# A fused two-block transformer kernel on Trainium2: the second convolution's products joined, high and low halves of the activations through one stationary block

## The chip, the cores and the metric

The kernel runs on one core of one Trainium2 chip. The metric is the device time of one execution in microseconds (us). Engines are named TensorE (PE, its weight loads PEld), VectorE (DVE), ScalarE (ACT), GpSimd (POOL) and SyncE (SP, which issues the weight DMAs).

## What is computed

The reference runs two transformer blocks over 256 tokens of width 1024, all in float32. The change lies in the second block, which is (cut):

```python
u = rms_norm(x, norm1_g[l])
proj = u @ w_in[l]
q, k, v, cb, cc, ch, ga, gb = jnp.split(proj, split_pts, axis=-1)   # cb, cc, ch: 512 columns each
...
y_a = neighbourhood_attention(q, k, v, rpb[l]) @ w_attn_branch[l]
y_b = short_gated_conv(cb, cc, ch, conv_w[l]) @ w_conv_branch[l]
merged = jax.nn.sigmoid(ga) * y_a + jax.nn.sigmoid(gb) * y_b
...
def short_gated_conv(cb, cc, ch, w):
    z = cc * ch
    zp = jnp.pad(z, ((0, 0), (1, 1), (0, 0)))
    conv = zp[:, :-2] * w[0] + zp[:, 1:-1] * w[1] + zp[:, 2:] * w[2]
    return cb * conv
```

## The kernel before, in words

Every float32 product is made of three products of a faster 32-bit type: both operands are split into a high part (rounded) and a low part (the rest), and high x high, high x low and low x high are summed in PSUM. ScalarE makes the high part of each weight piece (`split_hi`, L1105) and VectorE the low part (`split_lo`, L1524).

The weights stream through in 147 pieces of 128x2048 (1 MB), numbered by slot `s`. Each slot is one step of a loop that every engine runs over all slots, in program order; what an engine does in a slot stands in its block of code, and semaphores tie the engines. A piece is split two slots ahead (`AHEAD`), in rings of three buffers. The order around the change, in slots: q2 87 and 88, k2 89 and 90, v2 91 and 92, **cb2 93 and 94, cc2 95 and 96, ch2 97 and 98**, then four chunks of gates g2 (99 to 106), then the branch products ab2, cv2. A chunk of 512 columns takes two pieces, each over half of the 1024 input features; the first *opens* the PSUM banks and the second *closes* them.

PSUM has eight banks of 512 float32 words in each partition. `claim(key, b)` makes TensorE wait until bank `b` was drained by its last reader (semaphore `bank_drained<b>`); `ready` makes a reader wait until a bank was filled; `drain_of` counts it as drained. cb2, cc2 and ch2 have the form "feat" (features on the partitions): four tiles of 128 features x 256 tokens, two tiles in a bank. `stream` runs a piece in two halves, one bank each, with 24 matmuls of 256 columns per half (`three`, L402: weight high x activation high, weight high x activation low, weight low x activation high). Bank pairs (0, 1) and (2, 3) alternate by chunk: `b = 2 * pair[0] + half`, and `pair[0] ^= 1` when a chunk closes. cb2 so lies in banks 2 and 3, cc2 in 0 and 1, ch2 in 2 and 3, the first gates chunk in 0 and 1.

Between the two halves of a piece, `slot_middle` puts in the attention of the second block: a score block (`scores`, L801, banks 4 and 5) in slots 94 to 97 and a value block (`values2`, L838, bank 7) in slots 97 to 100, and after the pieces 96 to 99 a turn block (`prob_turn`, L816, banks 6 and 7). On VectorE the attention is `softmax_max` (L1696 reads banks 4 and 5 and adds the bias, L1701 takes the maximum), `softmax_divide` (L1717, L1719) and the low part `o_lo` of the values (L2109, which drains bank 7); on ScalarE it is `exps` (L1184), `prob_out` (L1216) and `o_hi` (L1474).

VectorE evacuates cb2 and cc2 (L2080: a bank half times the row scale) after `split_lo` of its slot and before the slot's `softmax_max`, and ch2 (L2130: z2 = ch2 x cc2) as the last of slot 98, after that slot's `softmax_divide`.

The MLP pieces have the form "wide" (`stream_wide`, L586 and L591): one stationary block of weights meets the high and low halves of the activations side by side, 512 columns, in one bank; then the low part of the weights meets the high activations, 256 columns, into the bank's first half. The two halves of a bank are added afterwards: ScalarE copies the second halves of two banks (L1227), VectorE adds the first halves (L1901).

Of the kernel before, what the change touches and what calls it, by code (L numbers as in the profile page):

```python
# [29 lines left out]
ALU = mybir.AluOpType  # L30
# [3 lines left out]
P = 128  # L34
# [78 lines left out]


TURN_AT = {18: 0, 19: 1, 20: 2, 21: 3, 22: 4, 24: 5}
SILU_AT = {19: (2, 3), 21: (4,), 23: (5,), 25: (6,)}
TAPS_AT = {9: 0, 13: 1, 15: 2, 17: 3, 19: 4, 21: 5, 23: 6, 25: 7}
LAST_TAPS = 26
# [37 lines left out]
def build(nc, w_stream, w_kv, x_in, params_in, table_in, onehot_in, gate_bias_in, post_in, rpb_in,  # L156
# [3 lines left out]
    with ctx:  # L160
# [154 lines left out]
        def sem(name):  # L315
            return ctx.enter_context(nc.semaphore(name))
# [19 lines left out]
        conv_tap0, conv_tapped, conv_silu, z_first_silu = (  # L336
            sem("conv_tap0"), sem("conv_tapped"), sem("conv_silu"), sem("z_first_silu"))
        z_last_silu, skip_ready = sem("z_last_silu"), sem("skip_ready")
        cum_ready = sem("cum_ready")
        ndt_ready = sem("ndt_ready")  # L340
        decay_scaled, own_ready, x_state_ready = sem("decay_scaled"), sem("own_ready"), sem("x_state_ready")
# [25 lines left out]
        def emptied(eng, key):  # L367

            eng.wait_ge(drained[where[key][0]], where[key][1] + 1)
# [12 lines left out]
        def _(pe):  # L382
            def claim(key, b):

                if uses[b]:
                    pe.wait_ge(drained[b], uses[b])
                where[key] = [b, uses[b], None]
                uses[b] += 1

            def fill_of(key):  # L390

                b = where[key][0]
                fills[b] += 1
                where[key][2] = (filled[b], fills[b])
                return filled[b], 1

            def three(o, act_hi, act_lo, hi, lo, weights_still, first, last):
# [3 lines left out]
                for n, (still, moving) in enumerate(pairs):  # L401
# [7 lines left out]
            hi_first = {"wo": (12, "mix0"),  # L409
                        "wo2": (24, "mix1"), "mi2": (28, "norm3")}  # L410
            crossed = ("wo", "mo", "wo2", "mo2")
            pair = [0]

            def stream_hi_first(s):
# [156 lines left out]
                    where[("q", 0, 1)][2] = (piece_done, 2)  # L571
                    pair[0] ^= 1

            def stream_wide(s):

                name, form, chunk, part, opens, closes = slots[s]
                hi, lo = w_hi[s % SPLIT_RING], w_lo[s % SPLIT_RING]

                def cols(kt, i):
                    return slice(kt * 512 + i * P, kt * 512 + i * P + P)  # L580

                def highs(i):
                    if opens:
                        claim((name, chunk, i), 4 * (chunk % 2) + i)
                    for kt in range(4):
                        pe.matmul(ps[:, 4 * (chunk % 2) + i, :], hi[:, cols(kt, i)], ht[:, :, 4 * part + kt, :],  # L586
                                  start=opens and kt == 0, stop=False, skip_group_check=True)

                def lows(i):
                    for kt in range(4):  # L590
                        ins = pe.matmul(ps[:, 4 * (chunk % 2) + i, 0:TOK], lo[:, cols(kt, i)],  # L591
                                        ht_hi[:, 4 * part + kt, :], start=False, stop=closes and kt == 3,
                                        skip_group_check=True)
                    return ins

                together = 2 if closes else 4
                for first in range(0, 4, together):
                    for i in range(first, first + together):
                        highs(i)
                    if first == 0:  # L600
                        pe.wait_ge(lo_ready, s + 1)
                    for i in range(first, first + together):
                        ins = lows(i)
                        if closes and i < 3:
                            ins.then_inc(*fill_of((name, chunk, i)))
                ins.then_inc(piece_done, 1)
                if closes:
                    where[(name, chunk, 3)][2] = (piece_done, s + 1)
# [32 lines left out]
            def stream(s, between=None):  # L641
# [1 line left out]
                hi, lo = w_hi[s % SPLIT_RING], w_lo[s % SPLIT_RING]  # L643
                pe.wait_ge(hi_ready, s + 1)
                if form == "wide" and chunk:
                    stream_wide(s)
                    return
                pe.wait_ge(lo_ready, s + 1)
                if name in hi_first and chunk == 0 and form != "acc":
# [437 lines left out]
        def _(act):  # L1087
# [168 lines left out]
            for s in range(SLOTS):  # L1256
# [213 lines left out]
                if 0 <= s - 97 < 4:  # L1470
                    a = s - 97
                    r, g = a // 2, a % 2
                    ready(act, ("a2o", a))
                    act.activation(o2_hi[:, 2 * g:2 * g + 2, r * P:r * P + P],  # L1474
                                   ps[:, 7, 0:2 * P].rearrange("p (h i) -> p h i", h=2),
                                   ACT.Copy).then_inc(ot_hi_ready, 1)
                if 0 <= s - 96 < 4:
                    prob_out("a2", s - 96, 0, prob_t2)
                    prob_out("a2", s - 96, 1, prob_t2)
                if s == S_CH2 + 2:  # L1480

                    emptied(act, ("ch2", 0, 0)), emptied(act, ("ch2", 0, 1))
                    for i in range(4):
                        act.activation(acc2[:, i, :], z2[:, i, 1:1 + TOK], ACT.Copy,
                                       scale=conv_w2[:, 1, i:i + 1]).then_inc(tap2_ready, 1)
# [3 lines left out]
                if name == "g2" and closes:  # L1489
                    for r in range(RT):  # L1490
                        key = ("g2", chunk, r)
                        ready(act, key)
                        if chunk == 0 and r == 0:

                            act.wait_ge(prob_ready, 12)
                            emptied(act, ("cb2", 0, 1)), emptied(act, ("cc2", 0, 1))
                        act.activation(gates2[:, r, chunk * 512:chunk * 512 + 512], ps[:, bank(key), :],
                                       ACT.Sigmoid, scale=row_scale[:, 0, r:r + 1]).then_inc(*drain_of(key))
                if s == S_WO2 - 1:
# [12 lines left out]
        def _(dve):  # L1512
# [381 lines left out]
            def feed_forward(name, c):  # L1894
# [11 lines left out]
                for half in range(2):  # L1906
# [2 lines left out]
                    dve.tensor_tensor(ff_lo[:, f:f + 2, :], ff_sum[half][:, :, :],  # L1909
                                      ff_hi[:, f:f + 2, :].bitcast(F32), ALU.subtract).then_inc(ff_ready, 1)  # L1910

            def mix(j, dest, first, second):

                for r in range(RT):
                    for n in range(2):
                        a = dest[:, r, n * 512:n * 512 + 512]
                        b = dest[:, r, D + n * 512:D + n * 512 + 512]
                        key = (second, n, r)
                        ready(dve, key)
                        own, other = (a, b) if j == 0 else (b, a)  # L1920
                        dve.tensor_tensor(own, ps[:, 2 * n + r, :], own, ALU.mult).then_inc(*drain_of(key))
                        emptied(dve, key)
                        emptied(dve, (first, n, r))
                        dve.tensor_tensor(a, a, b, ALU.add).then_inc(mixed_ready, 1)  # L1924
# [26 lines left out]
            for s in range(SLOTS):  # L1951
# [123 lines left out]
                if name in ("cb2", "cc2") and closes:  # L2075
                    dest, power = (cb2, 0) if name == "cb2" else (cc2, 1)
                    for half in range(2):
                        key = (name, 0, half)
                        ready(dve, key)
                        dve.tensor_tensor(dest[:, 2 * half:2 * half + 2, :],  # L2080
                                          ps[:, bank(key), :].rearrange("p (a b) -> p a b", a=2),
                                          scale_row[:, power, :].unsqueeze(1).to_broadcast([P, 2, TOK]),
                                          ALU.mult).then_inc(*drain_of(key))

                if name in ("q2", "k2") and closes:
                    part_of = 0 if name == "q2" else 1
# [34 lines left out]
                    softmax_divide(s - 95, logit2, 8, False)  # L2121

                if name == "ch2" and closes:
                    emptied(dve, ("cc2", 0, 0)), emptied(dve, ("cc2", 0, 1))
                    dve.wait_ge(pads_zero, 2)
                    for half in range(2):
                        key = ("ch2", 0, half)
                        ready(dve, key)
                        f = slice(2 * half, 2 * half + 2)
                        dve.tensor_tensor(z2[:, f, 1:1 + TOK],  # L2130
                                          ps[:, bank(key), :].rearrange("p (a b) -> p a b", a=2),
                                          cc2[:, f, :], ALU.mult).then_inc(*drain_of(key))
                if s == S_CH2 + 3:
                    for i in range(4):
                        dve.wait_ge(tap2_ready, i + 1)
                        for tap in (0, 2):
                            link(dve.scalar_tensor_tensor(acc2[:, i, :], z2[:, i, tap:tap + TOK],
                                                          conv_w2[:, tap, i:i + 1], acc2[:, i, :],
                                                          ALU.mult, ALU.add))
                    emptied(dve, ("cb2", 0, 0)), emptied(dve, ("cb2", 0, 1))  # L2140
                    dve.tensor_tensor(acc2[:, :, :], acc2[:, :, :], cb2[:, :, :], ALU.mult).then_inc(conv2_ready, 1)
                if s == S_CH2 + 4:
                    dve.wait_ge(co_hi_ready, 1)
# [209 lines left out]
```

## Time and profile before

| | us |
|---|---|
| median of 3 runs (lowest to highest) | 931.22 (930.92 to 931.59) |
| the profiled execution's own time | 930.91 |
| its span in the trace | 929.1 |
| TensorE busy | 922.3 (99%) |
| weight loads busy | 798.5 (86%) |
| VectorE busy | 656.6 (71%) |
| ScalarE busy | 522.7 (56%) |
| GpSimd busy | 59.1 (6%) |
| DMA share of 16 engines, hardware queue | 47.2% |

The span is the traced part of the profiled execution; the sum of the prediction is made against that execution. Matmuls are pipelined: a matmul's own duration is longer than the distance to the start of the next, so their pace is read from starts, and from counts over a stretch.

### The profile page before, as it was taken

The numbers are of one execution on the slowest core, as the hardware profiler recorded it, in microseconds if no ns is written. First come the engines' busy times: TensorE is split into PE (matmuls) and PEld (weight loads), VectorE is DVE, ScalarE is ACT, GpSimd is POOL, SyncE is SP. The second block draws the span as 40 slices with busy tenths as digits, with TensorE's granted clock in tenths as the row PEclk, the third lists the DMA queues.
The fourth block names the chain that finished last, engine by engine and source line by source line (L and its number), as shares of the span: only waits on it lengthen the run. The fifth ranks groups of instructions, "written<-read, shape, count | busy, mean of one in ns | idle before, by whom it ended". The sixth has DMA issues, their size and how long they took to land.

```text
span 929.1 us, 13131 instructions
## 1 busy us (share of the span) xinstructions
PE 922.3 (99%) x5264; PEld 798.5 (86%) x5264; DVE 656.6 (71%) x972; ACT 522.7 (56%) x735; POOL 59.1 (6%) x59
## 2 busy tenths in 40 slices
PE   9999999999999999999999999999999999999998
PEld 7988999988888888888888888899888898888886
DVE  6669989988889655788775446768655768876333
ACT  7457787767874733665554335756644356554330
POOL 1000000112231000000004400000000000000000
PEclk9999999999999999999999999999999999999999
DMA  8943334453227575445557854553355445455541
GB/s 308 369 147 127 101 127 142 177 166 128 91 91 249 171 281 181 181 171 184 196 194 224 255 186 177 181 181 137 136 184 206 168 139 210 182 186 222 187 176 46
DMA packets 25277, 166.51 MB, mean 179 GB/s; under 512 B 2986, under 2 KB 3114, under 8 KB 6912
## 3 DMA queue, kind: packets, MB, share of 16 engines
q1 hardware_dynamic: 22464, 156.12, 47.2%
q0 software_dynamic: 2752, 9.54, 3.4%
q8 instruction: 42, 0.69, 0.3%
q14 instruction: 19, 0.16, 0.0%
HBM read 164.57 MB, written 1.08 MB: 178 GB/s over the span
## 4 chain that ended last, share of the span: by engine, by line
PE 93%; DVE 4%; ACT 2%; issue 1%; DMA 0%; SPq 0%; DVEq 0%; ACTq 0%
PE ps L402 60%; PE ps L586 11%; PE ps L591 6%; PE ps L517 2%; PE ps L872 1%; PE ps L801 1%; PE ps L816 1%; PE ps L918 1%; PE ps L665 1%; PE ps L524 1%; PE ps L892 1%; PE ps L881 1%; PE ps L826 1%; DVE conv_acc L1783 1%; DVE gates L1924 1%
## 5 line engine op out<-in xcount | busy, mean ns | idle before, releaser
L1524 DVE TENSOR_TENSOR w_lo<-raw,w_hi 128x2048 fp32r<-128x2048 f32 (+1 forms) x144 | 330.1, 2297 | 183.6 <-ACT w_hi L1105 183.6
L1105 ACT ACTIVATE w_hi<-raw 128x2048 fp32r<-128x2048 f32 (+1 forms) x144 | 274.0, 1906 | 186.7 <-PE ps L402 160.2
L402 PE MATMUL ps<-w_hi,ht 128*128 128x512 f32 (+1 forms) x576 | 183.3, 390 | 0.0
L402 PE MATMUL ps<-ht,w_hi 128*128 128x256 f32 x800 | 148.1, 286 | 0.0
L402 PEld LDWEIGHTS ps<-ht,w_hi 128*128 128x128 f32 x800 | 124.3, 191 | 4.6 <-issue 4.6
L402 PEld LDWEIGHTS ps<-w_hi,ht 128*128 128x128 f32 x576 | 107.6, 188 | 22.3 <-issue 1.0
L402 PE MATMUL ps<-ht,w_lo 128*128 128x256 f32 x400 | 113.1, 283 | 0.0
L402 PE MATMUL ps<-w_lo,ht 128*128 128x512 f32 (+1 forms) x288 | 111.0, 385 | 0.0
L586 PE MATMUL ps<-ht,w_hi 128*128 128x512 f32 x448 | 109.6, 391 | 0.0
L402 PE MATMUL ps<-w_hi,ff_hi 128*128 128x512 f32 x256 | 99.7, 389 | 0.0
L402 PE MATMUL ps<-w_lo,ff_hi 128*128 128x512 f32 x256 | 99.6, 389 | 0.0
L402 PE MATMUL ps<-w_hi,ff_lo 128*128 128x512 f32 x256 | 99.6, 389 | 0.0
L586 PEld LDWEIGHTS ps<-ht,w_hi 128*128 128x128 f32 x448 | 81.5, 189 | 15.2
L402 PEld LDWEIGHTS ps<-ht,w_lo 128*128 128x128 f32 x400 | 76.6, 191 | 0.0
L402 PEld LDWEIGHTS ps<-w_lo,ht 128*128 128x128 f32 x288 | 54.1, 188 | 10.4
L591 PEld LDWEIGHTS ps<-ht,w_lo 128*128 128x128 f32 x448 | 59.3, 191 | 3.3
L591 PE MATMUL ps<-ht,w_lo 128*128 128x256 f32 x448 | 60.3, 282 | 0.0
L402 PEld LDWEIGHTS ps<-w_hi,ff_lo 128*128 128x128 f32 x256 | 48.1, 188 | 10.1
L402 PEld LDWEIGHTS ps<-w_lo,ff_hi 128*128 128x128 f32 x256 | 48.1, 188 | 9.9
L402 PEld LDWEIGHTS ps<-w_hi,ff_hi 128*128 128x128 f32 x256 | 48.1, 188 | 9.8
L1783 DVE SCALAR_TENSOR_TENSOR conv_acc<-conv_in,params,conv_acc 128x256 f32<-128x256 f32 x128 | 52.0, 481 | 0.0
L1227 ACT ACTIVATE ff_sum<-ps 128x512 f32<-128x512 f32 x30 | 17.8, 596 | 37.7 <-PE ps L591 36.9
(305 smaller groups left out, 1200.7 us busy)
## 6 DMA issues: line engine op xcount, KB each, us to landing
raw<-in_w_stream SPq DMA_DIRECT2D x143, 1024.0 KB, 4.8
bias<-rel_scratch POOLq DMA_DIRECT2D x1, 3072.0 KB, 22.6
bias<-in_rpb POOLq DMA_DIRECT2D x16, 128.0 KB, 8.3
raw<-in_w_kv SPq DMA_DIRECT2D x2, 864.0 KB, 8.4
x_first<-in_x_in SPq DMA_DIRECT2D x2, 512.0 KB, 4.0
raw<-in_w_stream SPq DMA_DIRECT2D x2, 512.0 KB, 6.2
gates<-in_gate_bias POOLq DMA_DIRECT2D x4, 256.0 KB, 5.6
gates<-in_gate_bias POOLq DMA_DIRECT2D x2, 512.0 KB, 7.7
```

What stands on the lines that cost most here:

```text
L402: ins = pe.matmul(o, still, moving, start=first and n == 0, stop=last and n == 2, skip_group_check=True)
L517: pe.matmul(ps[:, bank0 + r, :], ht_hi[:, 4 * part + kt, tokens], w[:, kt * 512:kt * 512 + 512], start=part == 0 and kt == 0 and m == 0, s ...
L524: ins = pe.matmul(ps[:, bank0 + r, :], ht_lo[:, 4 * part + kt, tokens], hi[:, kt * 512:kt * 512 + 512], start=False, stop=part == 1 and kt ...
L586: pe.matmul(ps[:, 4 * (chunk % 2) + i, :], hi[:, cols(kt, i)], ht[:, :, 4 * part + kt, :], start=opens and kt == 0, stop=False, skip_group ...
L591: ins = pe.matmul(ps[:, 4 * (chunk % 2) + i, 0:TOK], lo[:, cols(kt, i)], ht_hi[:, 4 * part + kt, :], start=False, stop=closes and kt == 3, ...
L665: pe.matmul(ps[:, 2 * n + r, :], a_hi[:, kt, r * P:r * P + P], w[:, cols], start=kt == 0 and m == 0, stop=False, skip_group_check=True)
L801: ins = pe.matmul(ps[:, 4 + e, h * TOK:h * TOK + TOK], q_tile(h)[rows, (1 - r) * P:(1 - r) * P + P], k_tile(h)[rows, :], start=True, stop= ...
L816: ins = pe.transpose(ps[:, 6 + half, o:o + P], logit[a % 2][:, 2 * half + h, jt * P:jt * P + P], flip)
L1105: act.activation(split_home(s)[0][:, 0:width(s)], raw[s % RAW_RING][:, 0:width(s)], ACT.Copy).then_inc(hi_ready, 1)
L1227: act.activation(ff_sum[half][:, :, :], ps[:, b:b + 2, TOK:2 * TOK], ACT.Copy).then_inc(lows_out, 1)
L1524: dve.tensor_tensor(lo[:, 0:width(s)], raw[s % RAW_RING][:, 0:width(s)], hi[:, 0:width(s)].bitcast(F32), ALU.subtract).then_inc(lo_ready, 1)
L1783: ins = dve.scalar_tensor_tensor(acc_of(c)[:, i, :], conv_in[k][:, i, tap:tap + TOK], conv_w[:, tap, f:f + 1], acc_of(c)[:, i, :], ALU.mul ...
```

## The change

The three chunks cb2, cc2 and ch2 take the wide form: each chunk uses four banks (0 to 3), one for each tile of 128 features, 16 matmuls of 512 columns and 16 of 256 in a piece, in two halves of two banks with the attention block still between them. ScalarE copies the low halves of two banks into the chunk's own SBUF tile (cb2, cc2, or acc2 for ch2) and counts `later_lows`. VectorE's new `add_lows` adds the banks' first halves onto it, one instruction a bank, waits for their end, and then multiplies as before, now from SBUF. `conv_scaled` and `gated2` take the place of the bank counts that later readers waited for. The bank pair is no longer turned over by these three chunks. (`name == "q"` and `WIDE_Q` have no effect: q is not in `joined_later`.)

```diff
@@ tensor @@
+            joined_later = ("cb2", "cc2", "ch2",)
...
-            def stream_wide(s):
+            def stream_wide(s, bank_of, together, between=None):
...
                 def highs(i):
                     if opens:
-                        claim((name, chunk, i), 4 * (chunk % 2) + i)
+                        claim((name, chunk, i), bank_of(i))
                     for kt in range(4):
-                        pe.matmul(ps[:, 4 * (chunk % 2) + i, :], hi[:, cols(kt, i)], ht[:, :, 4 * part + kt, :],
+                        pe.matmul(ps[:, bank_of(i), :], hi[:, cols(kt, i)], ht[:, :, 4 * part + kt, :],
...
+                    if first == 0 and together == 2 and between:
+                        between(s)
...
                 if form == "wide" and chunk:
-                    stream_wide(s)
+                    stream_wide(s, lambda i: 4 * (chunk % 2) + i, 2 if closes else 4)
+                    return
+                if name in joined_later:
+                    stream_wide(s, lambda i: (WIDE_Q if name == "q" else range(4))[i], 2, between)
+                    if name == "q" and closes:
+                        pair[0] ^= 1
                     return
@@ scalar @@
+                if name in ("cb2", "cc2", "ch2") and closes:
+                    dest = {"cb2": cb2, "cc2": cc2, "ch2": acc2}[name]
+                    for half in range(2):
+                        ready(act, (name, 0, 2 * half)), ready(act, (name, 0, 2 * half + 1))
+                        act.activation(dest[:, 2 * half:2 * half + 2, :], ps[:, 2 * half:2 * half + 2, TOK:2 * TOK],
+                                       ACT.Copy).then_inc(later_lows, 1)
                 if 0 <= s - 96 < 4:
                     prob_out("a2", s - 96, 0, prob_t2)
...
                 if s == S_CH2 + 2:
-                    emptied(act, ("ch2", 0, 0)), emptied(act, ("ch2", 0, 1))
+                    act.wait_ge(gated2, 2)
...
-                            emptied(act, ("cb2", 0, 1)), emptied(act, ("cc2", 0, 1))
+                            act.wait_ge(conv_scaled, 4)
@@ vector @@
+            def add_lows(name, dest, half, first):
+                dve.wait_ge(later_lows, first + half + 1)
+                for i in range(2 * half, 2 * half + 2):
+                    key = (name, 0, i)
+                    dve.tensor_tensor(dest[:, i, :], ps[:, bank(key), 0:TOK], dest[:, i, :],
+                                      ALU.add).then_inc(*drain_of(key))
+                emptied(dve, (name, 0, 2 * half)), emptied(dve, (name, 0, 2 * half + 1))
...
                     for half in range(2):
-                        key = (name, 0, half)
-                        ready(dve, key)
-                        dve.tensor_tensor(dest[:, 2 * half:2 * half + 2, :],
-                                          ps[:, bank(key), :].rearrange("p (a b) -> p a b", a=2),
-                                          scale_row[:, power, :].unsqueeze(1).to_broadcast([P, 2, TOK]),
-                                          ALU.mult).then_inc(*drain_of(key))
+                        add_lows(name, dest, half, 0 + 2 * power)
+                        v = dest[:, 2 * half:2 * half + 2, :]
+                        dve.tensor_tensor(v, v, scale_row[:, power, :].unsqueeze(1).to_broadcast([P, 2, TOK]),
+                                          ALU.mult).then_inc(conv_scaled, 1)
...
-                    emptied(dve, ("cc2", 0, 0)), emptied(dve, ("cc2", 0, 1))
+                    dve.wait_ge(conv_scaled, 4)
                     dve.wait_ge(pads_zero, 2)
                     for half in range(2):
-                        key = ("ch2", 0, half)
-                        ready(dve, key)
                         f = slice(2 * half, 2 * half + 2)
-                        dve.tensor_tensor(z2[:, f, 1:1 + TOK],
-                                          ps[:, bank(key), :].rearrange("p (a b) -> p a b", a=2),
-                                          cc2[:, f, :], ALU.mult).then_inc(*drain_of(key))
+                        add_lows("ch2", acc2, half, 4)
+                        dve.tensor_tensor(z2[:, f, 1:1 + TOK], acc2[:, f, :], cc2[:, f, :],
+                                          ALU.mult).then_inc(gated2, 1)
```

How the rows of the built program move at the two places that the prediction speaks of. First TensorE from the turn block behind piece 98 (`prob_turn`, which reads `logit`) to the first gates piece, before; `w_hi` and `w_lo` are the buffers of a weight piece, numbers behind a name are the program's own.

```order
L816 MATMUL ps<-params,logit_0_149 128x128 [waits bank_drained6,prob_ready]
L816 MATMUL ps<-params,logit_0_149 128x128 x3
L816 MATMUL ps<-params,logit_0_149 128x128 [waits bank_drained7]
L816 MATMUL ps<-params,logit_0_149 128x128 x3
L402 MATMUL ps<-w_hi_52,ht 128x512 [waits bank_drained0,lo_ready,hi_ready]
```

And now, with the end of piece 98 in the wide form ahead of it:

```order
L590 MATMUL ps<-ht,w_hi_54 128x512 x8
L595 MATMUL ps<-ht,w_lo_57 128x256 x8
L826 MATMUL ps<-params,logit_0_149 128x128 [waits bank_drained6,prob_ready]
L826 MATMUL ps<-params,logit_0_149 128x128 x3
L826 MATMUL ps<-params,logit_0_149 128x128 [waits bank_drained7]
L826 MATMUL ps<-params,logit_0_149 128x128 x3
L405 MATMUL ps<-w_hi_52,ht 128x512 [waits bank_drained2,lo_ready,hi_ready]
```

The first gates matmul waited for bank 0 and now waits for bank 2, which is ch2's third. Second, VectorE from the low split in slot 94 over cb2 to the first softmax reads (`logit`), before:

```order
L1524 TENSOR_TENSOR w_lo_55<-raw_49,w_hi_52 128x2048 [waits hi_ready]
L2080 TENSOR_TENSOR cb_143<-ps,scale_row 128x512 [waits bank_filled2]
L2080 TENSOR_TENSOR cb_143<-ps,scale_row 128x512 [waits piece_done]
L1696 SCALAR_TENSOR_TENSOR logit_0_149<-ps,bias_153 128x512 [waits bank_filled4,bias2_masked]
L1696 SCALAR_TENSOR_TENSOR logit_0_149<-ps,bias_153 128x512 [waits bank_filled5]
```

And now:

```order
L1540 TENSOR_TENSOR w_lo_55<-raw_49,w_hi_52 128x2048 [waits hi_ready]
L1932 TENSOR_TENSOR cb_143<-ps,cb_143 128x256 [waits later_lows]
L1932 TENSOR_TENSOR cb_143<-ps,cb_143 128x256
L2104 TENSOR_TENSOR cb_143<-cb_143,scale_row 128x512 [waits bank_drained1,bank_drained0]
L1932 TENSOR_TENSOR cb_143<-ps,cb_143 128x256 [waits later_lows]
L1932 TENSOR_TENSOR cb_143<-ps,cb_143 128x256
L2104 TENSOR_TENSOR cb_143<-cb_143,scale_row 128x512 [waits bank_drained3,bank_drained2]
L1712 SCALAR_TENSOR_TENSOR logit_0_149<-ps,bias_153 128x512 [waits bank_filled4,bias2_masked]
L1712 SCALAR_TENSOR_TENSOR logit_0_149<-ps,bias_153 128x512 [waits bank_filled5]
```

Four adds stand ahead of the softmax reads that were not there, and the adds wait for ScalarE's copies (`later_lows`) where the multiply waited for TensorE.

## Rows read from the trace of the kernel before

**Rows 1.** The page: span, busy times, chain by engine, the largest weight-load group.

```profile
span 929.1 us, 13131 instructions
...
PE 922.3 (99%) x5264; PEld 798.5 (86%) x5264; DVE 656.6 (71%) x972; ACT 522.7 (56%) x735; POOL 59.1 (6%) x59
...
PE 93%; DVE 4%; ACT 2%; issue 1%; DMA 0%; SPq 0%; DVEq 0%; ACTq 0%
...
L402 PEld LDWEIGHTS ps<-ht,w_hi 128*128 128x128 f32 x800 | 124.3, 191 | 4.6 <-issue 4.6
```

**Rows 2.** Chain in order of time: start, us, engine, tile, line, count.

```profile
610.45 8.63 PE ps L402 x72
```

**Rows 3.** Timeline of TensorE, a closing wide piece of the MLP: start, us, count.

```profile
799.63 2.00 PE L586 MATMUL ps<-ht,w_hi 128*128 128x512 f32 x8
801.47 1.12 PE L591 MATMUL ps<-ht,w_lo 128*128 128x256 f32 x8
802.43 2.00 PE L586 MATMUL ps<-ht,w_hi 128*128 128x512 f32 x8
804.27 1.11 PE L591 MATMUL ps<-ht,w_lo 128*128 128x256 f32 x8
805.22 3.82 PE L586 MATMUL ps<-ht,w_hi 128*128 128x512 f32 x16
```

**Rows 4.** Timelines of ScalarE and VectorE, the MLP's evacuation; last, VectorE's group by form.

```profile
805.47 0.60 ACT L1227 ACTIVATE ff_sum<-ps 128x512 f32<-128x512 f32 x1 [2.19 <-PE ps L591]
...
806.10 0.76 DVE L1901 TENSOR_TENSOR ff_sum<-ps,ff_sum 128x256 f32<-128x256 f32 x2 [0.50 <-ACT ff_sum L1227]
806.96 0.69 DVE L1904 SCALAR_TENSOR_TENSOR ff_sum<-ff_sum 128x512 f32<-128x512 f32 x1
...
L1901 DVE TENSOR_TENSOR ff_sum<-ps,ff_sum 128x256 f32<-128x256 f32 x8 | 3.0, 417 | 0.5 <-ACT ff_sum L1227 0.5
```

**Rows 5.** Timeline of TensorE, slots 95 to 99: score, turn and first gates instructions.

```profile
626.01 1.14 PE L801 MATMUL ps<-qk_t 64*128 64x256 f32 x8
...
641.93 1.13 PE L801 MATMUL ps<-qk_t 64*128 64x256 f32 x8
...
645.96 1.04 PE L816 MATMUL ps<-params,logit 128*128 128x128 f32 x8
...
653.80 1.03 PE L816 MATMUL ps<-params,logit 128*128 128x128 f32 x8
654.59 0.48 PE L402 MATMUL ps<-w_hi,ht 128*128 128x512 f32 x1
```

**Rows 6.** Timelines of VectorE and, last row, ScalarE, slots 94 to 98.

```profile
623.25 0.69 DVE L2080 TENSOR_TENSOR cb<-ps,scale_row 128x512 f32<-128x512 f32 x1 [2.11 <-PE ps L402]
623.86 1.28 DVE L1696 SCALAR_TENSOR_TENSOR logit<-ps,bias 128x512 f32<-128x512 f32 x2
...
638.14 1.29 DVE L1696 SCALAR_TENSOR_TENSOR logit<-ps,bias 128x512 f32<-128x512 f32 x2 [0.18 <-PE ps L816]
...
644.33 0.42 DVE L2109 TENSOR_TENSOR o_lo<-ps,o_hi 128x256 fp32r<-128x256 f32 x1
647.03 1.29 DVE L1696 SCALAR_TENSOR_TENSOR logit<-ps,bias 128x512 f32<-128x512 f32 x2 [2.27 <-PE ps L816]
...
653.76 1.14 DVE L1719 TENSOR_SCALAR logit<-logit,soft 128x256 f32<-128x256 f32 x4
654.81 1.28 DVE L2130 TENSOR_TENSOR z<-ps,cc 128x512 f32<-128x512 f32 x2
...
651.87 0.36 ACT L1474 ACTIVATE o_hi<-ps 128x256 fp32r<-128x256 f32 x1
```

**Rows 7.** Timeline at the end of the first mix: VectorE releases TensorE.

```profile
371.38 0.69 DVE L1924 TENSOR_TENSOR gates<-gates 128x512 f32<-128x512 f32 x1
...
372.13 0.66 PE L743 MATMUL ps<-params,gates 128*128 128x128 f32 x4 [0.20 <-DVE gates L1924]
```

**Rows 8.** Busy times of the stretch 611 to 655 us; last columns: clock, DMA share, GB/s.

```profile
611.00:655.00 44.00, 44.00 (x374) 41.45 (x373) 32.16 (x49) 24.65 (x51) 0.00 (x0) 1.00 0.41 146
```

More of the change, by code:

```diff
@@ L115 @@
 TURN_AT = {18: 0, 19: 1, 20: 2, 21: 3, 22: 4, 24: 5}
+WIDE_Q = (4, 5, 2, 3)
 SILU_AT = {19: (2, 3), 21: (4,), 23: (5,), 25: (6,)}
@@ L338, in build @@
         z_last_silu, skip_ready = sem("z_last_silu"), sem("skip_ready")
+        conv_scaled, gated2 = sem("conv_scaled"), sem("gated2")
+        later_lows = sem("later_lows")
         cum_ready = sem("cum_ready")
@@ L590, in lows @@
                     for kt in range(4):
-                        ins = pe.matmul(ps[:, 4 * (chunk % 2) + i, 0:TOK], lo[:, cols(kt, i)],
+                        ins = pe.matmul(ps[:, bank_of(i), 0:TOK], lo[:, cols(kt, i)],
                                         ht_hi[:, 4 * part + kt, :], start=False, stop=closes and kt == 3,
@@ L594, in lows @@
                     return ins
-                together = 2 if closes else 4
                 for first in range(0, 4, together):
@@ L2139, in _ @@
                                                           ALU.mult, ALU.add))
-                    emptied(dve, ("cb2", 0, 0)), emptied(dve, ("cb2", 0, 1))
                     dve.tensor_tensor(acc2[:, :, :], acc2[:, :, :], cb2[:, :, :], ALU.mult).then_inc(conv2_ready, 1)
```

## The prediction

> **What bounds the kernel now.** I read the page first. TensorE is busy 922.3 of 929.1 us, and the chain that ended last runs 93% over it [rows 1], so a microsecond of TensorE is a microsecond of the kernel, wherever it falls. Then the waits of TensorE: in the stretch of the change (610 to 655 us) none on a bank or a weight piece is listed, only pauses before blocks of other instructions. So the change can win there by fewer or cheaper matmuls, and lose by each wait that it brings; both are worked out below. The later waits (the eight gate pieces behind it have a nearly idle VectorE) absorb nothing, since TensorE stays the bound.
>
> **The matmuls.** A convolution piece has 48 matmuls of 256 columns. The chain gives 72 of them in 8.63 us, 0.120 us each [rows 2], so 5.76 us a piece. The new form is that of the MLP's wide pieces: 16 of 512 columns and 16 of 256. There 8 of 512 take 801.47 - 799.63 = 1.84 us (0.230 each) and 8 of 256 take 0.96 us; two halves make 2.80 + 2.79 = 5.59 us [rows 3]. The width of 512 costs nearly two of 256, and I gain 0.17 us a piece, 1.0 us over six. The columns are the same in both forms, 12,288 a piece, so no more is to be had than what each matmul costs beside its columns. TensorE's granted clock is 1.00 of full, its upper level of 2.4 GHz, over this stretch [rows 8]; I price no change of it.
>
> The Trainium skill (TensorE: Matmul & The Clock Gate, in Part 1, "Wait — 56ns, not 53.3ns?") gives a start-to-start time of the columns at 2.4 GHz plus about 2.5 ns, that is 109 and 216 ns; by it 96 fewer matmuls would give 0.24 us in all. The trace's 120 and 230 ns differ from both, and the trace decides.
>
> **The evacuation.** Before, one VectorE instruction of 128x512 reads a bank pair's half (0.61 us from start to start) and frees the bank. Now a half goes through ScalarE (a copy of 128x512, 0.60 us), two VectorE adds of 128x256 with a wait for their own end (806.10 to 806.96, 0.86 us; one lasts 0.42), and then the multiply of 0.61 as before [rows 4]. Extra per half: 0.60 us on ScalarE, which has the room (24.65 us of work in 44 [rows 8]), and 0.86 us on VectorE; of six halves 3.6 and 5.2 us. Added DMAs: none; SP's and POOL's queues are not touched. What lies behind them on VectorE is the softmax of the attention, and behind that TensorE's score and turn blocks, which stand in the middle and at the end of each piece. So I follow VectorE.
>
> *First place, the second score block (piece 95).* Before it starts at 626.01 [rows 5]. It writes banks 4 and 5, which VectorE frees with the two softmax reads that start at 623.86 and take 1.28 us (625.14): 0.9 us in hand [rows 6]. Now: two and a half cheaper pieces bring the block's natural start to 626.01 - 0.42 = 625.59. The second half of cb2, ready at 623.25 [rows 6], is ready 0.34 earlier, at 622.91. Behind it stand the copy 0.60, the adds 0.86, the multiply 0.61, the softmax reads 1.28 and some 0.06 from a VectorE end to the next TensorE start (VectorE ends at 372.07, TensorE starts at 372.13 [rows 7]): 626.32. TensorE waits 0.73 us. Bounds: nothing (if the second half's copy overlapped more than I think) and 1.1 us (if each of copy, adds and multiply cost its full duration plus a handover).
>
> *The same for cc2.* VectorE's reads for the third scores move from 638.14 to some 639.4, but the fourth score block needs them only at 641.9 [rows 5, 6]; covered, with 1.2 us to spare. VectorE then has slack of 2.27 us before 647.03, which waits for the turn block at 645.96 [rows 5, 6], and takes up the 1.3 us. The turn block itself needs bank 7, freed by the o_lo instruction at 644.33 plus 1.3, about 646.0; its second half wants it at 646.3: 0.3 to spare, the thinnest cover in the chain.
>
> *Second place, the gates' first chunk (piece 99).* Before, it opens banks 0 and 1, two pieces old. Now the three chunks no longer turn the bank pair over and it opens bank 2, which ch2 fills to the end of piece 98. In between lies only a turn block of 0.79 us (653.80 to 654.59 [rows 5]). By ScalarE alone that would be a short wait, but VectorE is late there already: from 647.03 to 654.81 it has no gap before the ch2 product [rows 6], and its start there hangs on the turn block at 645.96. That block moves by -0.85 (five pieces) + 0.73 = -0.12 us, so ch2's work starts at 654.69. ScalarE's copy of the first half is long done (it is free at 652.2 [rows 6]); then adds 0.86, multiply 0.61, the first add of the second half 0.42, handover 0.06: bank 2 is free at 656.64. TensorE wants it at 654.59 - 0.12 - 0.17 = 654.30 and waits 2.34 us. Bank 3 follows 0.4 us later and is wanted only after twelve matmuls. Bounds: 0.3 us if VectorE were free (copy 0.60, add 0.42, handover 0.06, less the 0.79 of the block), 3.2 us if VectorE came still later by the bank 7 above. I take 2.34, since the rows show VectorE without a gap.
>
> The Trainium skill (Perfetto Trace Analysis, "Matmuls" under "Optimizing Tensor Performance") asks that independent matmul groups rotate through different PSUM banks, so that one's evacuation overlaps the next one's matmuls. The order of banks before keeps to that, the one after breaks it at piece 99; no run here yet shows at what price.
>
> After piece 99 nothing is tight: the gates' pieces have VectorE and ScalarE mostly idle, and the attention branch opens bank 0, which is freed a half piece before, and bank 1 six matmuls later.
>
> **Sum.** -1.02 (matmuls) + 0.73 + 2.34 = +2.05 us. The profiled execution took 930.91 us (span 929.1 and 1.8 around it); 932.96 with the change. The median of the runs shown is 0.31 above that execution, so 933.3 us.
>
> **Rivals.**
> (a) *Only the wait at piece 99.* The score block finds its banks free; VectorE's start at piece 99 is then 0.73 earlier: 932.5 us. For it: 0.7 us is a sum of five small terms. Against: each has its row.
> (b) *Not slower: VectorE has caught up at piece 99.* If its gap before the ch2 product were there (the last softmax divide done early, since the ScalarE part is off its path), bank 2 would be free 1.1 us after the end of piece 98; the wait is 0.3 us, and with the score wait covered the change comes to -0.7: 930.5 us. It decides if VectorE reaches ch2 before 652.6, so that adds and multiply of the first half (1.47 us) are behind it when ScalarE has copied the second (654.1). Against: it reaches it at 654.81 before, and nothing in front of it gets shorter.
> (c) *A third wait.* Bank 7 is late for the turn block at 645.96, which then holds back everything that hangs on it: with 0.5 us there and a little more in the other two 934.3 us.
> (d) *Faster: matmuls are paced by their number.* A weight load shows 191 ns against a pitch of 120 [rows 1, 2], so if a load set the pace whatever the width, 16 fewer at 0.120 us would save 1.92 us a piece, 11.5 in all; less the waits, some 922.8 us. Against: the wide pieces show 0.230 for 512 columns. The Trainium skill (Perfetto Trace Analysis, "Identifying the Most-Contended Engine") judges TensorE's headroom by the busy share of its weight loads, which is this rival's reading; that share falls here without the time falling with it, I hold.
> (e) *The joined matmuls gain nothing here* (0.240 for 512 columns, as two of 256), so that the change doesn't do what it is built for: only the waits stay. The score wait is then 0.65 us, and VectorE reaches ch2 that much later than before, at 655.46; bank 2 is free at 657.41 instead of a start at 654.59: +2.8, 934.0 us.
>
> **How the numbers follow.** Chances: forecast 0.55, (a) 0.15, (b) 0.10, (c) 0.12, (d) 0.03, (e) 0.05. A measurement of this kernel tells apart about 0.2%, 1.9 us: slower means over 933.1. The forecast's own spread, 932.6 to 933.9, lies across that; I give 0.42 of its 0.55 to slower. Slower: 0.42 + 0.12 + 0.05 = 0.59; within: 0.13 + 0.15 + 0.10 = 0.38; faster: 0.03. The range reaches from 931.4, between (b) and (a), to 934.8, a little above (c) and (e).
>
> **What would show it.** In the profile after: the L590 and L595 rows (the new lines of the wide form) at 1.84 and 0.96 us for eight; a wait of TensorE on VectorE before the second score block, some 0.7 us; no gap of VectorE between the fourth softmax's reads and the ch2 adds; a gap of TensorE of about 2.3 us ahead of the first gates matmul, released by the first add of ch2's second half. The prediction is wrong if that gap is under 1 us, if a gap stands before the second turn block, or if a piece takes other than 5.6 us.

## The result and the profile after

| | before | changed |
|---|---|---|
| median of 6 runs, us | 931.06 (930.92 to 931.59) | 935.09 (933.55 to 935.97) |
| ratio, 95% interval | 1 | 1.0041 (1.0029 to 1.0053) |
| profiled execution, own time / span | 930.91 / 929.1 | 935.03 / 933.2 |

The change costs 4.0 us, where 2.1 were forecast (931.22 to 933.3), and the median lies 0.3 us above the range. The page of the changed kernel, span and busy times:

```profile
span 933.2 us, 12962 instructions
...
PE 923.3 (99%) x5168; PEld 794.5 (85%) x5168; DVE 660.2 (71%) x984; ACT 525.8 (56%) x741; POOL 59.6 (6%) x59
```

Against [rows 1], TensorE has 96 matmuls fewer and is busy 1 us longer, and the span has grown by 4.1 us: some 3 us of it are gaps, and some of the busy time has become slower. The pieces themselves do what was forecast. TensorE's timeline over cb2's closing piece (start, us, count), to be read against [rows 3]:

```profile
615.87 2.00 PE L590 MATMUL ps<-ht,w_hi 128*128 128x512 f32 x8
617.71 1.11 PE L595 MATMUL ps<-ht,w_lo 128*128 128x256 f32 x8
618.75 1.14 PE L811 MATMUL ps<-qk_t 64*128 64x256 f32 x8
```

Eight of 512 columns in 1.84 us. The score block starts at 618.75 and not at 619.00, after one and a half pieces. Next, TensorE at the two places of the prediction, which answers to [rows 5]:

```profile
626.51 1.13 PE L811 MATMUL ps<-qk_t 64*128 64x256 f32 x8 [0.83 <-DVE logit L1712]
...
646.07 1.04 PE L826 MATMUL ps<-params,logit 128*128 128x128 f32 x8
...
653.76 1.03 PE L826 MATMUL ps<-params,logit 128*128 128x128 f32 x8
656.96 0.47 PE L405 MATMUL ps<-w_hi,ht 128*128 128x512 f32 x1 [2.16 <-DVE acc L1932]
```

And VectorE, which answers to [rows 6]:

```profile
623.62 0.75 DVE L1932 TENSOR_TENSOR cb<-ps,cb 128x256 f32<-128x256 f32 x2 [1.79 <-ACT cb L1491]
624.48 0.69 DVE L2104 TENSOR_TENSOR cb<-cb,scale_row 128x512 f32<-128x512 f32 x1
625.09 1.28 DVE L1712 SCALAR_TENSOR_TENSOR logit<-ps,bias 128x512 f32<-128x512 f32 x2
...
645.88 0.41 DVE L2131 TENSOR_TENSOR o_lo<-ps,o_hi 128x256 fp32r<-128x256 f32 x1
647.15 1.29 DVE L1712 SCALAR_TENSOR_TENSOR logit<-ps,bias 128x512 f32<-128x512 f32 x2 [0.85 <-PE ps L826]
...
653.87 1.14 DVE L1735 TENSOR_SCALAR logit<-logit,soft 128x256 f32<-128x256 f32 x4
654.93 0.75 DVE L1932 TENSOR_TENSOR acc<-ps,acc 128x256 f32<-128x256 f32 x2
655.78 0.69 DVE L2151 TENSOR_TENSOR z<-acc,cc 128x512 f32<-128x512 f32 x1
656.39 0.75 DVE L1932 TENSOR_TENSOR acc<-ps,acc 128x256 f32<-128x256 f32 x2
```

Both waits are there, released by the instructions named ahead: the score block starts at 626.51 (forecast 626.32), the first gates matmul at 656.96 (forecast 656.64), 2.37 us later than the 654.59 of [rows 5]. VectorE's slack before the turn block shrank from 2.27 to 0.85 us and held. But 2.4 us is not 4.1. What is missing stands right behind the gap, in TensorE's timeline:

```profile
657.49 0.97 PE L405 MATMUL ps<-w_hi,ht 128*128 128x512 f32 x2
658.26 0.63 PE L405 MATMUL ps<-w_lo,ht 128*128 128x512 f32 x1
658.68 1.06 PE L405 MATMUL ps<-w_hi,ht 128*128 128x512 f32 x2
659.54 0.63 PE L405 MATMUL ps<-w_lo,ht 128*128 128x512 f32 x1
...
661.46 1.09 PE L848 MATMUL ps<-prob_t,v 128*64 128x128 f32 x16
```

and in the busy times by stretch of the same trace (us of the stretch, busy time of PE, PEld, DVE, ACT and POOL, then the granted clock, DMA share, GB/s):

```profile
654.00:657.00 3.00, 0.84 (x9) 0.63 (x7) 2.90 (x9) 2.99 (x4) 0.00 (x0) 1.00 0.84 268
657.00:661.00 4.00, 4.00 (x11) 3.17 (x12) 3.04 (x3) 0.39 (x1) 0.00 (x0) 0.57 0.15 61
661.00:665.00 4.00, 4.00 (x30) 3.01 (x29) 0.42 (x1) 0.38 (x1) 0.00 (x0) 1.00 0.70 266
...
657.00:657.50 0.50, 0.50 (x3) 0.42 (x4) 0.40 (x2) 0.39 (x1) 0.00 (x0) 1.00 1.16 492
658.00:661.00 3.00, 3.00 (x9) 2.35 (x8) 2.14 (x1) 0.00 (x0) 0.00 (x0) 0.50 0.00 0
```

From one matmul of 512 columns to the next it takes 0.43 us instead of 0.23 (659.54 - 658.68 = 0.86 for two). The granted clock is 0.57 over these four us and 1.00 before and after. From 658 to 661 us it is 0.50, its lower level of 1.2 GHz; it fell behind TensorE's standstill of 2.2 us, half a microsecond or more after TensorE had started again at 656.96. One of the six runs took 933.55 us, with a mean granted clock of 1.000; in the five others it was 0.998.

### The profile page after: what moved, and what is told of

The parts are those of the page before. It is cut to its first block, busy times and chain, and to the rows that moved or that the text cites. A ratio compares the mean times of both kernels' runs of the same rounds, so it can differ in the third digit from the quotient of the medians.

```text
span 933.2 us, 12962 instructions
## 1 busy us (share of the span) xinstructions
PE 923.3 (99%) x5168; PEld 794.5 (85%) x5168; DVE 660.2 (71%) x984; ACT 525.8 (56%) x741; POOL 59.6 (6%) x59
## 4 chain that ended last, share of the span: by engine, by line
PE 92%; DVE 5%; ACT 2%; issue 1%; DMA 0%; SPq 0%; DVEq 0%; ACTq 0%
PE ps L405 57%; PE ps L590 13%; PE ps L595 7%; PE ps L521 2%; PE ps L882 1%; PE ps L811 1%; PE ps L826 1%; PE ps L928 1%; PE ps L675 1%; PE ps L528 1%; PE ps L902 1%; PE ps L891 1%; PE ps L836 1%; DVE conv_acc L1799 1%; DVE gates L1948 1%
## 5 line engine op out<-in xcount | busy, mean ns | idle before, releaser
L590 PE MATMUL ps<-ht,w_hi 128*128 128x512 f32 x544 | 134.5, 393 | 0.0
L590 PEld LDWEIGHTS ps<-ht,w_hi 128*128 128x128 f32 x544 | 98.6, 188 | 19.9 <-issue 1.5
L405 PE MATMUL ps<-ht,w_hi 128*128 128x256 f32 x608 | 112.5, 286 | 0.0
L405 PEld LDWEIGHTS ps<-ht,w_hi 128*128 128x128 f32 x608 | 94.5, 191 | 3.1 <-issue 3.1
L405 PE MATMUL ps<-ht,w_lo 128*128 128x256 f32 x304 | 85.9, 283 | 0.0
L595 PEld LDWEIGHTS ps<-ht,w_lo 128*128 128x128 f32 x544 | 72.3, 191 | 4.2
L595 PE MATMUL ps<-ht,w_lo 128*128 128x256 f32 x544 | 73.6, 282 | 0.0
L405 PEld LDWEIGHTS ps<-ht,w_lo 128*128 128x128 f32 x304 | 58.2, 191 | 0.0
```

The lines of the kernel that those rows point to most:

```text
L405: ins = pe.matmul(o, still, moving, start=first and n == 0, stop=last and n == 2, skip_group_check=True)
L590: pe.matmul(ps[:, bank_of(i), :], hi[:, cols(kt, i)], ht[:, :, 4 * part + kt, :], start=opens and kt == 0, stop=False, skip_group_check=True)
L595: ins = pe.matmul(ps[:, bank_of(i), 0:TOK], lo[:, cols(kt, i)], ht_hi[:, 4 * part + kt, :], start=False, stop=closes and kt == 3, skip_gro ...
```

## The experiments

Theory at this point: the change costs two waits on VectorE, and the second also lowers TensorE's clock for a while. Rivals: the slow matmuls come of something else that happens at 657 us (the DMA share there is 0.84 just before, and 0.15 during); or the wide form and its evacuation cost more in places that two traces don't show. Times are medians beside runs of the kernel before on the same chip; that kernel had 931.05, 931.23 and 931.10 us in the three sets.

**The bank pair turned over at ch2**

```diff
-                    if name == "q" and closes:
+                    if name == "ch2" and closes:
                         pair[0] ^= 1
```

> The changed kernel, but the bank pair is turned over once more when ch2 closes, so that the first gates chunk opens bank 0 again. Theory (the loss is the wait for bank 2 at piece 99 and the lowered clock behind it, 57% of full over 657 to 661 us in the changed kernel's trace): the gates start at about 654.6 us of the span as before the change, no gap of TensorE there, clock at 1.00, and the time is 931.0 us, as before the change. Rival 1 (the wide form of the pieces or the longer evacuation costs more elsewhere): 932.5 us or more with no gap at piece 99. Rival 2 (the clock falls there for another reason than the gap): 932.8 us, with the low clock still behind piece 98.

Measured: 931.98 us (931.82 to 933.23), ratio 1.0012 (1.0003 to 1.0021), clock 0.999 to 1.000 in all runs. So 3.1 us of the 4.0 are gone, but the expected 931.0 is missed by 1.0 and the gap isn't gone: the clock stayed up as the theory has it, but a wait is left. TensorE and VectorE of this run (its trace is of the slowest of the eleven runs, 933.23 us, and is 1.3 us late from the start of the stretch on, 611.51 for 610.20):

```profile
655.08 1.03 PE L826 MATMUL ps<-params,logit 128*128 128x128 f32 x8
656.82 0.47 PE L405 MATMUL ps<-w_hi,ht 128*128 128x512 f32 x1 [0.70 <-DVE acc L1932]
...
655.20 1.14 DVE L1735 TENSOR_SCALAR logit<-logit,soft 128x256 f32<-128x256 f32 x4
656.25 0.75 DVE L1932 TENSOR_TENSOR acc<-ps,acc 128x256 f32<-128x256 f32 x2
```

The turn block takes 0.79 us, so the gates could start at 655.87 and start at 656.82, once VectorE's first add on ch2 (656.25 + 0.4) has freed bank 0. I had overlooked that ch2 now fills all four banks: turned over or not, the gates' pair is ch2's, and the turn only decides whether its first or its second half is waited for.

**The first score block read ahead of cb2's second half** (with the pair turned over)

```diff
                     for half in range(2):
+                        if name == "cb2" and half == 1:
+                            dve.wait_ge(bias2_masked, 2)
+                            softmax_max("a2", 0, logit2, lambda half: bias2[:, 0, half:half + 3:2, :])
                         add_lows(name, dest, half, 0 + 2 * power)
...
-                if 0 <= s - 94 < 4:
+                if 0 < s - 94 < 4:
...
-                    if a == 0:
-                        dve.wait_ge(bias2_masked, 2)
```

> As the run with the pair turned over, and VectorE reads the first score block ahead of the second half of cb2 instead of behind it. Theory (VectorE's later softmax reads hold the second score block 0.8 us): that wait goes, all six pieces keep their 0.17 us, and the time is 930.2 us, 0.8 below the run before it and some 0.9 below the kernel before the change. Rival (the wait only moves, to a turn block or to the next score block): no faster than the run with the pair turned, 931.0 us.

Measured: 931.11 us (930.88 to 933.09), ratio 1.0003 (0.9994 to 1.0012). The step, 931.98 to 931.11, is 0.87 us where 0.8 was expected; both levels lie 0.9 to 1.0 higher than expected, by the wait for bank 0. No wait before a score block is left in its trace. One of its eleven runs, the 933.09, has a clock of 0.998. The first wait is priced: 0.8 to 0.9 us.

**The wait filled with matmuls**

```diff
+                    if s == S_G2:
+                        emptied(pe, ("a2s", 3, 0))
+                        for _ in range(8):
+                            pe.matmul(ps[:, 4, :], ht_hi[:, 0, 0:P], ht_hi[:, 0:2, :], start=True, stop=True,
+                                      skip_group_check=True)
                     stream(s, slot_middle)
```

> The changed kernel with eight matmuls of 512 columns, whose result is thrown away, ahead of the first gates piece, in a free bank; they take 8 x 0.23 = 1.84 us of the wait of 2.2 us. Theory (the low clock follows from TensorE standing still): the gates still start at about 657.0 us of the span, but the clock stays at 1.00 behind it, and the time is 933.3 us, 1.8 below the changed kernel's 935.1. Rival (the slow matmuls at 657 to 661 us have to do with what the other engines and the DMAs do then): the time stays 935.1 us and the granted clock there stays low.

Measured: 933.50 us (933.29 to 933.75), clock 1.000 in all eight runs. The timeline of TensorE and the busy times of the stretch behind:

```profile
654.51 2.09 PE L1007 MATMUL ps<-ht 128*128 128x512 f32 x8
656.92 0.47 PE L405 MATMUL ps<-w_hi,ht 128*128 128x512 f32 x1 [0.32 <-DVE acc L1937]
...
657.00:661.00 4.00, 4.00 (x29) 3.06 (x30) 3.00 (x3) 0.39 (x2) 0.00 (x0) 1.00 0.09 39
```

The gates start where they did in the changed kernel (656.92 and 656.96), the other engines and the DMAs do the same, and only TensorE's standstill is filled: 1.6 us come back. So the slow matmuls follow from the standstill. Work that is thrown away makes the changed kernel faster.

**Three matmuls instead of eight**

```diff
-                        for _ in range(8):
+                        for _ in range(3):
```

> As the run with eight thrown-away matmuls ahead of the first gates piece, with three: 0.7 us of the wait is filled, and some 1.5 us of gap is left. The gates start at about 657.0 us as in the changed kernel. If a gap of 1.5 us leaves the clock alone: 933.5 us in all runs. If it lowers it as one of 2.2 us does: 935.1 us. In between: some runs of each.

Measured: 933.46 us (933.20 to 934.03), clock 0.999 to 1.000 in all ten runs. The gap left was

```profile
657.10 0.47 PE L405 MATMUL ps<-w_hi,ht 128*128 128x512 f32 x1 [1.47 <-DVE acc L1937]
```

and a gap of 1.5 us leaves the clock alone here.

**The changed kernel once more**, unedited.

> The changed kernel once more, beside the two others, to see how its runs divide. Theory: in most of its runs the clock falls behind the gap (mean granted clock 0.998 of full, 935.1 us), in a few it doesn't (1.000, 933.5 us), as one of six did. Rival (its runs scatter around 935 with no tie to the clock): times between the two, clock of no help.

Measured: 934.95 us; single runs 934.95, 935.07 and 935.13 with a clock of 0.998, 933.38 and 933.60 with 1.000. With the six runs above, the clock fell in 8 of 11, and the times form two groups 1.5 us apart. The profiled execution is one in which it did not fall, which gives the same kernel both ways. TensorE's timeline, then the busy times of the stretch:

```profile
657.03 0.47 PE L405 MATMUL ps<-w_hi,ht 128*128 128x512 f32 x1 [2.17 <-DVE acc L1932]
657.33 0.40 PE L405 MATMUL ps<-w_lo,ht 128*128 128x512 f32 x1
657.57 0.63 PE L405 MATMUL ps<-w_hi,ht 128*128 128x512 f32 x2
...
659.96 1.09 PE L848 MATMUL ps<-prob_t,v 128*64 128x128 f32 x16
...
663.84 1.03 PE L826 MATMUL ps<-params,logit 128*128 128x128 f32 x8
...
657.00:661.00 4.00, 3.97 (x29) 3.04 (x29) 3.11 (x3) 0.46 (x1) 0.00 (x0) 1.00 0.16 66
```

From the first gates matmul to the value block it takes 2.93 us here and 661.46 - 656.96 = 4.50 us with the low clock: 1.57 us. The turn block behind piece 99 gives the same over a longer stretch: it starts at 663.84 here, 6.81 us behind the first gates matmul, and in the trace with the low clock 8.42 us behind it:

```profile
665.38 1.03 PE L826 MATMUL ps<-params,logit 128*128 128x128 f32 x8
```

**ch2's evacuation ahead of the last softmax divide** (the changed kernel, the two blocks of `if` in VectorE's slot swapped)

```diff
-                if 0 <= s - 95 < 4:
-                    softmax_divide(s - 95, logit2, 8, False)
-
                 if name == "ch2" and closes:
...
+                if 0 <= s - 95 < 4:
+                    softmax_divide(s - 95, logit2, 8, False)
```

> The changed kernel with ch2's evacuation on VectorE ahead of the last softmax divide instead of behind it, 1.3 us earlier. Theory (VectorE's queue sets when bank 2 is free; a gap of TensorE under one and a half us leaves the clock alone): bank 2 is free at about 655.6 us, the gap is about 1.1 us instead of 2.2, the clock stays at 1.00 and the time is 932.2 us. Rival 1 (any gap lowers the clock): gap 1.1 us and 1.8 us for the clock, 934.0 us. Rival 2 (ScalarE's copy sets it, not VectorE): gap and time unchanged, 935.1 us.

Measured: 932.23 us (932.02 to 932.82), ratio 1.0012 (1.0003 to 1.0021), clock 0.999 to 1.000. The gates start when VectorE's third add is done (655.22 + 0.4), and not when ScalarE's second copy is, which ends at 654.70:

```profile
655.78 0.47 PE L405 MATMUL ps<-w_hi,ht 128*128 128x512 f32 x1 [0.90 <-DVE acc L1932]
...
655.22 0.74 DVE L1932 TENSOR_TENSOR acc<-ps,acc 128x256 f32<-128x256 f32 x2
...
654.10 0.60 ACT L1491 ACTIVATE acc<-ps 128x512 f32<-128x512 f32 x1 [1.19 <-PE ps L595]
```

Rival (b) of the prediction had its place right (VectorE's standing at ch2 decides), and this edit buys 1.2 of the 2.0 us of wait that it names.

**The kernel before, with only the order of banks changed**

```diff
-                if closes:
+                if closes and name != "ch2":
                     pair[0] ^= 1
```

> The kernel before the change with one edit: the bank pair is not turned over when ch2 closes, so the first gates chunk opens bank 2, while all products and evacuations stay as they were. Theory (the order of banks alone brings a wait, and its length is set by where VectorE has got to): VectorE frees bank 2 at 654.8 + 0.7 = 655.5 us, the gates start at 655.6 instead of 654.6 us, the clock stays at 1.00, and the time is 932.1 us. Rival 1 (any gap lowers the clock): 933.9 us. Rival 2 (the order of banks is harmless without the longer evacuation): 931.1 us.

Measured: 932.21 us (932.02 to 932.92) beside 931.23, ratio 1.0010 (1.0001 to 1.0019), clock 0.999 to 1.000. The gates start 1.2 us later than in [rows 5] (the turn block some 0.2), released by the last reader of bank 2:

```profile
655.80 0.47 PE L402 MATMUL ps<-w_hi,ht 128*128 128x512 f32 x1 [0.81 <-DVE z L2130]
```

The order of banks alone costs 1.0 us without any wide form.

**A longer wait** (the pair turned over, and one wait added)

```diff
+                    if s == S_G2:
+                        pe.wait_ge(gated2, 2)
                     stream(s, slot_middle)
```

> The run with the pair turned over (no wait for a bank at piece 99), with one wait put in: TensorE starts the gates only when VectorE has finished ch2's product, at about 658.0 us of the span, a gap of some 3.4 us. Theory (after a long gap the clock is low for a while at the same price): 931.0 + 3.4 + 1.8 = 936.2 us, the granted clock low behind the gap in every run. Rival (the price of the low clock grows with the gap): over 937.5 us. If the clock does not fall: 934.4 us.

Measured: 936.23 us (935.97 to 936.39), ratio 1.0054 (1.0041 to 1.0067), clock 0.998 in all five runs. TensorE's timeline and the busy times:

```profile
658.33 0.50 PE L405 MATMUL ps<-w_hi,ht 128*128 128x512 f32 x1 [3.20 <-DVE z L2153]
...
658.00:659.50 1.50, 1.17 (x5) 0.99 (x6) 1.50 (x2) 0.00 (x0) 0.00 (x0) 1.00 0.00 0
659.50:663.00 3.50, 3.50 (x14) 2.40 (x13) 0.98 (x1) 0.00 (x0) 0.00 (x0) 0.54 0.40 103
...
666.73 1.03 PE L826 MATMUL ps<-params,logit 128*128 128x128 f32 x8
```

As forecast in the time: a gap a microsecond longer costs its own length more (936.23 against 935.09 us) and no more for the clock. From the first gates matmul to the turn block it is 8.40 us here, against 8.42 with the gap of 2.2 us and 6.81 with the clock up. The expectation calls the run with the pair turned over one without a wait at piece 99, which the run above contradicts; the 931.0 us that it starts from is right as the level without that wait (930.2 + 0.87). The clock falls over a microsecond after TensorE has started again, so it strikes work that runs densely.

**No waits** (the three edits together: pair turned over, first scores read earlier, ch2 ahead of the divide)

> The pair turned over, the first score block read ahead of cb2's second half, and ch2's evacuation ahead of the last softmax divide: the three edits together. Theory: in the two runs with the pair turned over TensorE still waited 0.9 us at piece 99, because ch2 now fills bank 0 as well as bank 2 and VectorE frees bank 0 only at 655.3 us; 1.3 us earlier that is covered (free at about 653.4, wanted at 653.8), no wait of TensorE is left between 610 and 660 us, and the whole saving of the matmuls shows: 931.05 - 1.0 = 930.05 us. Rival (the joined form saves nothing that reaches the end): 931.0 us, as before the change.

Measured: 930.20 us (929.93 to 930.42) beside 931.10 (930.89 to 931.88), ratio 0.9989 (0.9980 to 0.9998). No wait of TensorE on another engine is left in its trace between 609 and 663 us, and the gates follow the turn block at once:

```profile
652.90 1.03 PE L826 MATMUL ps<-params,logit 128*128 128x128 f32 x8
653.69 0.47 PE L405 MATMUL ps<-w_hi,ht 128*128 128x512 f32 x1
```

They start 0.90 us earlier than in the kernel before (654.59), which is the whole gain. This version is faster than both kernels, by 0.9 and some 4.8 us. Its ratio to the kernel before is clear of 1, but only just.

## Why the prediction was wrong

The direction was right, the size was not, and one step did most of it: in the paragraph on the matmuls, "I price no change of it", said of TensorE's clock. The same text forecast a standstill of 2.3 us at piece 99 and took the clock behind it for granted because the trace before shows it at 1.00 [rows 8]. That trace has no such standstill, so it could not show the clock's answer to one, and the unknown should have been bounded by a stretch at the lower level and kept as a rival. Its price is 1.5 us: 935.0 against 933.5 us within the changed kernel, and 1.6 us by filling the gap. The forecast of 933.3 us is close to what the changed kernel takes when the clock stays (933.38, 933.55, 933.60), but in part by luck: those runs lie 2.4 us above the kernel before (931.1), where the sum had 2.05. Its three terms were each off by 0.1 us towards too little loss, and the 931.22 us that it started from was 0.1 to 0.2 us too high.

The signs named ahead could not catch the error. The wait before the score block, the gap before the gates, VectorE without a gap before ch2, the missing gap at the second turn block and the 1.84 us for eight matmuls all came true in the trace of 935.03 us; none of them looks at the clock.

Point by point:

- *The matmuls, 1.02 us.* Measured 0.90 us where nothing waits (930.20 against 931.10, and the same in the trace), 0.15 us a piece and not 0.17. The 0.24 us that came of the Trainium skill (TensorE: Matmul & The Clock Gate, Part 1, "Wait — 56ns, not 53.3ns?") would have been too small; the rows of the wide pieces were the better source.
- *The second score block, 0.73 us.* 0.83 us of wait in the trace, 0.87 us by the run that takes it away.
- *The gates' first chunk, 2.34 us.* The trace has 2.16 us idle before TensorE's row (from 654.55, when the turn block's pace would have let it start, to 656.96, it is 2.4). VectorE's late place was the cause, as said: moved 1.2 us forward, it gives 1.3 us back (933.5 to 932.2).
- *Why that chunk waits.* The text put it down to the pair that is no longer turned over. That was half of it: with the pair turned, the gates still wait 0.9 us, since a chunk on four banks leaves no pair free. The sentence of the Trainium skill on rotating banks (Perfetto Trace Analysis, "Matmuls") holds here with its price: 1.0 us for the order of banks alone, 2.4 us and 1.5 for the clock with the longer evacuation.
- *Bank 7*, rival (c): `o_lo` starts at 645.88 (forecast 645.6), and the turn block at 646.07 shows no gap. The cover held.
- *Rivals (d) and (e)* fall with the pace of 0.230 us for 512 columns.

The ledger of the changed kernel, from the runs: 930.2 (no waits), +0.87 (scores), +0.9 (bank 0 at piece 99), +1.5 (bank 2 instead of bank 0, the difference of 931.98 and 933.5), +1.5 (clock) = 935.0; measured 935.09. Each step is the difference of two runs, so the sum closes by its making; what supports the steps is that the traces show the same lengths (0.83 us, 0.95 us, 1.46 us more of gap, 1.6 us).

## What to carry to other kernels

When TensorE is the bound and an edit saves a hundredth of a microsecond in each matmul of 512 columns (0.230 us for twice 0.120), look first at who frees the banks: here 1 us of matmuls was gained and 3 us of waits came with it, all of them removed by the three edits of order (the bank pair, the first softmax reads, ch2's evacuation). A forecast standstill of a dense TensorE can be dearer than its length, as the one of 2.2 us was here in 8 of 11 runs; give the clock behind it a term of its own, even where the profile at hand shows 1.00 throughout. And when a consumer gets late, let it free the banks first and do the rest later: moving ch2's evacuation ahead of a divide took no work away and gave 1.3 us back.

## What the runs showed of the hardware

- The granted clock fell behind a standstill of 2.2 us in 8 of 11 runs, and behind 3.2 us in 5 of 5; behind 1.5 us in none of 10, and with gaps of 0.7 to 0.9 us at piece 99 in one of 44 (the 933.09 us of the run with the scores read first, clock 0.998; it has no trace, so where its clock fell is not known). Each fall cost 1.5 to 1.6 us, at a pace of 0.43 instead of 0.23 us for 512 columns, whether the gap was 2.2 or 3.2 us. The Trainium skill (TensorE: Matmul & The Clock Gate, "Why this matters for your kernels") warns of idle gaps over about 3 us between bursts; here one of 2.2 us was enough in most runs.
- The fall comes late: with the gap of 2.2 us TensorE starts again at 656.96, the clock is 1.00 from 657.0 to 657.5 and 0.50 from 658 to 661; with the gap of 3.2 us it starts again at 658.33, and the clock is 1.00 to 659.5 and 0.54 from there to 663.
- What decides between the 8 and the 3 runs of the same kernel was not found: TensorE's two timelines up to the gap agree to 0.1 us.
